# The opening of a fused three-layer kernel, entered by halves of the tokens

## The chip, the cores and the metric

The kernel runs on one core of one Trainium2 chip. The metric is the device time of one execution in microseconds (us). The engines of the core are TensorE (PE, with its weight loads PEld), VectorE (DVE), ScalarE (ACT), GpSimd (POOL) and SyncE (SP); each works through its own instructions in order, and they meet through semaphores.

## The reference, cut to what matters

The program takes 512 tokens of 1024 values through three transformer layers. Only the first steps matter here:

```python
h = x                                            # (1, 512, 1024), f32
xn = _rms_norm(h, norm_g[0, 0])                  # x / sqrt(mean(x*x) + 1e-6) * gain
gq, gk, gv, glr, gr, nq, kc, vc, ks, vs, kw, vw, ng = split(xn @ w_in)     # w_in: 1024 x 2856
# _gla: glog = log_sigmoid(glr @ w_gate + b_gate) / 16, cumulated over chunks of 64 tokens
# q and k are scaled by exp of that sum; then the chunked linear attention
```

The last step of the program is an RMS norm of the result, stored as (1, 512, 1024).

## The kernel before, in words

**Precision.** Every dense product is taken in three passes: a value is split into hi (rounded for TensorE) and lo (the rest), and hi·hi, hi·lo and lo·hi are added (mm3, L2149 to L2151). For x the split is made while the turned tokens leave PSUM: ACT writes x_hi = gain · turned (L778) and DVE writes x_lo = gain · turned − x_hi (L1415). For weights ACT copies w_raw to w_hi (split_hi, L726) and DVE subtracts to get w_lo (split_lo, L1382).

**Weights.** They come in tiles of 1 MB through two slots of w_raw, w_hi and w_lo. SP issues the load of tile n when w_lo of tile n−2 is made. The first tiles are E_IN = small, gq, gk, gv0, kc, ... ("small" holds the low-rank gate columns and the NSA gate columns, and comes in two pieces of 320 and 192 KB; only its second 128 columns are used).

**Order of the opening.** SP issues the four token tiles of x (128 tokens each), then the weight tiles 0 to 3 (L544 on), of which tile 2 waits for w_lo of tile 0 and tile 3 for w_lo of tile 1, then the two compression weights cmp_w1. ACT first issues ten small loads of constant rows (L851), loads its table for Sqrt (L769), takes the sums of squares of x tiles 0 and 2, and then makes w_hi of tile 0 (L878). DVE takes the sums of squares of tiles 1 and 3 (L1500), copies the turned gain columns from PSUM (L1504), and writes the normed tokens m (L1409). POOL makes w_lo of tile 0 (L636).

TensorE (from L2355) does eight matmuls on constants whose result nobody reads ("warm", L2155; each shows as two records), turns the gain rows (L2359), does eight more, turns x tiles 0 and 1 into all eight PSUM banks (8 transposes each, L2164), does six more warm ones, and turns tiles 2 and 3. Bank k then holds rows 128k to 128k+127 of x, turned, for all 512 tokens, and ACT and DVE split it in eight pieces of 512 columns, a bank each.

**The dense units.** A unit is one 128-column half of a weight tile against all tokens: 24 matmuls of 512 columns. `dense(x, middle)` runs them in order of x; `e_unit(x)` maps x to (tile, half): x = 0 is small, x = 1 the first half of gq, x = 2 the second half of small, which is only four small transposes of gate columns already computed, x = 3 the second half of gq, x = 4 and 5 are gk, x = 6 and 7 gv0 (matmuls of 256 columns). Units 0 and 1 run ahead of their w_lo: the lo-weight matmuls (L2405) come some steps behind the others (L2399, L2400).

After unit 0 TensorE turns the other constant rows (later_consts, L2367), and after unit 1 it computes the gate products (gate_scores, L2417), which need ACT's copy of unit 0 and three small loads that ACT issues after the split of x (e_loaded: w_gate, gate_rows, cmp_w2).

**The chain behind the gate products.** In its program order ACT runs split_hi(2) and take_in(1), then gate_logs (L936 to L940: bias, Abs, Exp, Ln for two blocks, with two table loads). DVE's order is fixed too: split_lo(2), then gate_sums (L1519 to L1525: min, subtract, scale, scan, difference, for two blocks), then the addition of the gate bias (L1629, in step x = 3), and only then split_lo(3), which is the w_lo of gv0 that unit 6 waits for.

The rest of the program, up to its last token tile, is not touched. In the five later places where the tokens are turned (`head(p)`), it is already done by halves of 256 tokens: `turned_hi` (L795) and `turned_lo` (L1431) split pieces of 256 columns, two to a bank, and as ACT and DVE must not read one bank at the same time, each of them waits for the other every second piece.

**The end.** The last token tile is finished in two halves: ACT scales the first (L1372) and DVE the second (L2141). Each adds to final_done, and SP stores both, one after the other, when both are done (L603).

Of the kernel before, what the change touches and what calls it, by code (L numbers as in the profile page):

```python
# [20 lines left out]
F32 = mybir.dt.float32  # L21
# [6 lines left out]
P = 128  # L28
# [78 lines left out]
def program(nc, A, out):  # L107
# [23 lines left out]
    with ctx:  # L131
# [195 lines left out]
        tail_gained, tail_rstd = sem("tail_gained"), sem("tail_rstd")  # L327

# [46 lines left out]
        def x_base(p, a):  # L375

            return DK + 2 * DK * (p - 1) + DK * a
# [22 lines left out]
        def e_unit(x):  # L400

            return {1: (1, 0), 2: (0, 1)}.get(x, divmod(x, 2))
# [88 lines left out]
        def _(sp):  # L491
# [39 lines left out]
            for t in range(NT):  # L531
                sp.dma_start(h[:, t, :], A["x"][0, t * P:(t + 1) * P, :]).then_inc(x_loaded[t], 16)
            def load_e(i):
# [13 lines left out]
            for i in range(4):  # L547
                load_e(i)
# [51 lines left out]
            ends = [(t, slice(0, D)) for t in range(3)] + [(3, slice(0, D // 2)), (3, slice(D // 2, D))]  # L600
            for i, (t, cols) in enumerate(ends):
                sp.wait_ge(final_done, 5 if t == 3 else i + 1)
                sp.dma_start(out[0].rearrange("(t p) d -> p t d", p=P)[:, t, cols], m[:, t, cols]).then_inc(stored, 16)  # L603
            sp.wait_ge(stored, 16 * len(ends))
# [3 lines left out]
        def _(pool):  # L608
# [27 lines left out]
            nc.gpsimd.tensor_tensor(used[0], used[1], used[2].bitcast(F32), ALU.subtract).then_inc(w_lo_ready, 1)  # L636

# [80 lines left out]
        def _(act):  # L718
# [55 lines left out]
            def first_hi():  # L774
# [78 lines left out]
            def row_load(first, which, count, src):  # L853
                cload(const_rows[first:first + count, which, :], src)

            cload(const_rows[0:32, 0, :], A["norm_g"].rearrange("l (f two) (k p) -> two (l f) k p", two=2, p=P)[0], gains_loaded)
            row_load(0, 1, 8, A["norm_mix_2"][0].rearrange("(k p) -> k p", p=P))
            row_load(8, 1, 8, A["norm_ffn_2"][0].rearrange("(k p) -> k p", p=P))
            row_load(16, 1, 8, A["c_2"][0].rearrange("(k p) -> k p", p=P))
            row_load(24, 1, 48, A["b_ada_2"][0].rearrange("(k p) -> k p", p=P))  # L860
            row_load(72, 1, 16, A["o_ln_g"][0].rearrange("(k p) -> k p", p=P))
            row_load(0, 2, 16, A["o_ln_b"][0].rearrange("(k p) -> k p", p=P))
            row_load(16, 2, 2, A["gla_b_gate"][0].rearrange("(k p) -> k p", p=P))
            row_load(18, 2, 4, A["gla_norm"][0])
            row_load(22, 2, 32, A["nsa_cmp_pos"][0].rearrange("x (a b) d -> (x a) (b d)", b=2))

# [4 lines left out]
            for t in (0, 2):  # L871
                act.wait_ge(x_loaded[t], 16)
                root_of(t, t, h[:, t, :], m[:, t, :])
                act.wait_ge(x_squares, t // 2 + 1)
                nc.scalar.activation(root[:, t + 1:t + 2], ss[:, t + 1:t + 2], ACT.Sqrt,
                                     bias=small[:, 22:23]).then_inc(squares, 1)
# [3 lines left out]
            first_hi()  # L880
            split_hi(1, 1, loaded(1), 0)
# [490 lines left out]
            nc.scalar.activation(m[:, 3, first], m[:, 3, first], ACT.Copy, scale=rstd[:, 11:12]).then_inc(final_done, 1)  # L1372
# [3 lines left out]
        def _(dve):  # L1376
# [34 lines left out]
            def first_lo():  # L1411
# [734 lines left out]
        def _(pe):  # L2146
# [6 lines left out]
            def warm(count):  # L2153
                for _ in range(count):
                    nc.tensor.matmul(ps[:, 7, 3 * P:4 * P], ones[:, :], ident[:, :], start=True, stop=True)  # L2155
# [813 lines left out]
```

## Time and profile before

| | |
|---|---|
| time, median of 3 runs | 1993.37 us (1993.0 to 1993.6) |
| profiled execution, its own time | 1993.1 us |
| its span, first to last instruction | 1991.3 us |
| TensorE busy | 1975.5 us, 99% of the span |
| DVE / ACT / POOL busy | 1019.7 / 694.5 / 404.9 us |
| chain that ended last | PE 94%, DVE 3%, ACT 2% |

The span is measured inside the program; the time has about 1.8 us more around it. In the timeline the columns are the start in us from the span's start, the duration in us of the merged stretch, the engine, the line, the operation and what it writes and reads, the count, and in brackets how long the engine had stood idle and who ended that. Matmuls are pipelined: each shows its whole latency (0.39 us for one of 512 columns), while the next starts 0.23 us later, so work is counted from start to start.

### The profile page before, as it was taken

To read this page: it belongs to the slowest core of one execution; us is meant where nothing else is said; L and a number is where in the kernel's file an instruction comes from. 1 tells how busy PE (TensorE), PEld (TensorE's weight loads), DVE (VectorE), ACT (ScalarE), POOL (GpSimd) and SP (SyncE) were. 2 spreads that over 40 slices of the span, in tenths; PEclk is the share of its full clock that TensorE was granted. 3 is DMA by queue.
4 is the path that set the end of the run, shared out by engine and by line. 5 is a ranking of instruction groups with operands and counts; after the bars stand their busy time and mean duration, and the time that the engine had idled before them with its cause. 6 is when DMAs were issued, how large, how long until landed. Compare 5 with 4: busy or idle time off the path is not lost.

```text
span 1991.3 us, 27158 instructions
## 1 busy us (share of the span) xinstructions
PE 1975.5 (99%) x11044; PEld 1656.8 (83%) x11044; DVE 1019.7 (51%) x1391; ACT 694.5 (35%) x1008; POOL 404.9 (20%) x212
## 2 busy tenths in 40 slices
PE   9999999999999999999999999999999999999998
PEld 7878888888888888889888888888877888888887
DVE  5468758357345336626727535642543664322435
ACT  6357643122124323315312212534434252222222
POOL 1000007686600101000669661000000200000000
PEclk9999999999999999999999999999999999999999
DMA  6221134444333232232445442232221223323231
GB/s 198 74 61 44 46 114 159 157 139 153 123 104 117 84 97 85 85 113 89 148 140 167 148 146 87 85 106 76 70 80 64 86 84 106 102 99 106 84 106 64
DMA packets 135032, 208.91 MB, mean 105 GB/s; under 512 B 6346, under 2 KB 105864, under 8 KB 134920
## 3 DMA queue, kind: packets, MB, share of 16 engines
q1 hardware_dynamic: 125952, 180.37, 28.0%
q0 software_dynamic: 6912, 25.17, 3.8%
q10 hardware_dynamic: 2056, 1.76, 0.3%
q8 instruction: 85, 1.39, 0.3%
q14 instruction: 27, 0.22, 0.0%
HBM read 205.18 MB, written 2.10 MB: 104 GB/s over the span
## 4 chain that ended last, share of the span: by engine, by line
PE 94%; DVE 3%; ACT 2%; issue 0%; POOL 0%; ACTq 0%; POOLq 0%
PE ps L2149 28%; PE ps L2151 28%; PE ps L2150 28%; PE ps L2210 1%; PE ps L2600 1%; PE ps L2203 1%; PE ps L2202 1%; PE ps L2611 1%; PE ps L2700 1%; PE ps L2173 1%; PE ps L2792 1%; PE ps L2155 0%; DVE m L1460 0%; PE ps L2589 0%; PE ps L2588 0%
## 5 line engine op out<-in xcount | busy, mean ns | idle before, releaser
L1382 DVE TENSOR_TENSOR w_lo<-w_raw,w_hi 128x2048 fp32r<-128x2048 f32 x149 | 349.9, 2349 | 569.2 <-ACT w_hi L726 569.2
L2149 PE MATMUL ps<-x_hi,w_hi 128*128 128x512 f32 x1240 | 487.8, 393 | 0.4 <-DVE w_lo L1382 0.4
L2151 PE MATMUL ps<-x_hi,w_lo 128*128 128x512 f32 x1240 | 482.9, 389 | 0.0
L2150 PE MATMUL ps<-x_lo,w_hi 128*128 128x512 f32 x1240 | 482.8, 389 | 0.0
L726 ACT ACTIVATE w_hi<-w_raw 128x2048 fp32r<-128x2048 f32 x151 | 288.9, 1913 | 536.0 <-PE ps L2151 434.9
L2149 PEld LDWEIGHTS ps<-x_hi,w_hi 128*128 128x128 f32 x1240 | 233.3, 188 | 50.0 <-issue 2.5
L2151 PEld LDWEIGHTS ps<-x_hi,w_lo 128*128 128x128 f32 x1240 | 232.8, 188 | 49.1
L2150 PEld LDWEIGHTS ps<-x_lo,w_hi 128*128 128x128 f32 x1240 | 233.0, 188 | 46.3
L2149 PE MATMUL ps<-w_hi,h_hi 128*128 128x512 f32 x688 | 267.8, 389 | 0.0
L2151 PE MATMUL ps<-w_hi,h_lo 128*128 128x512 f32 x688 | 267.7, 389 | 0.0
L2150 PE MATMUL ps<-w_lo,h_hi 128*128 128x512 f32 x688 | 267.6, 389 | 0.0
L2151 PEld LDWEIGHTS ps<-w_hi,h_lo 128*128 128x128 f32 x688 | 129.2, 188 | 27.0
L2150 PEld LDWEIGHTS ps<-w_lo,h_hi 128*128 128x128 f32 x688 | 129.2, 188 | 26.8
L2149 PEld LDWEIGHTS ps<-w_hi,h_hi 128*128 128x128 f32 x688 | 129.2, 188 | 26.5
L684 POOL TENSOR_SCALAR ada_w<-ada_w,cols 128x1024 f32<-128x1024 f32 x42 | 144.5, 3440 | 2.7 <-DMA ada_w<-in_w_ada 0.6
L1125 ACT ACTIVATE work<-ps 128x512 f32<-128x512 f32 x64 | 38.2, 599 | 234.6 <-PE ps L2151 211.2
L685 POOL TENSOR_TENSOR ada_acc<-ada_acc,ada_w 128x1024 f32<-128x1024 f32 x42 | 114.9, 2735 | 3.5
L1770 DVE TENSOR_TENSOR work<-work 128x512 f32<-128x512 f32 x64 | 76.2, 1191 | 70.7 <-ACT work L1125 70.7
L2149 PE MATMUL ps<-w_hi,x_hi 128*128 128x256 f32 (+1 forms) x288 | 95.7, 332 | 0.0
L2150 PE MATMUL ps<-w_lo,x_hi 128*128 128x256 f32 (+1 forms) x288 | 95.1, 330 | 0.0
L2151 PE MATMUL ps<-w_hi,x_lo 128*128 128x256 f32 (+1 forms) x288 | 95.0, 330 | 0.0
L713 POOL TENSOR_TENSOR gate_t<-gate_t 128x512 f32<-128x512 f32 x8 | 13.9, 1776 | 358.1 <-DVE gate_t L2047 358.1
(404 smaller groups left out, 2695.5 us busy)
## 6 DMA issues: line engine op xcount, KB each, us to landing
w_raw<-in_ffn_w SPq DMA_DIRECT2D x64, 1024.0 KB, 5.4
ada_w<-in_w_ada POOLq DMA_DIRECT2D x48, 512.0 KB, 4.1
w_raw<-in_w_ffn_in SPq DMA_DIRECT2D x22, 1024.0 KB, 5.1
w_raw<-in_w_in SPq DMA_DIRECT2D x20, 1024.0 KB, 5.4
w_raw<-in_o_w_in SPq DMA_DIRECT2D x16, 1024.0 KB, 5.4
w_raw<-in_w_ffn_out SPq DMA_DIRECT2D x11, 1024.0 KB, 4.9
w_raw<-in_e_w_in SPq DMA_DIRECT2D x9, 1024.0 KB, 5.4
w_raw<-in_o_w_out SPq DMA_DIRECT2D x8, 1024.0 KB, 4.8
```

The source lines that it names most:

```text
L684: chain.link(nc.gpsimd.tensor_scalar(ada_w[:, s, :], ada_w[:, s, :], c_col[:, k:k + 1], None, ALU.mult))
L685: chain.link(nc.gpsimd.tensor_tensor(ada_acc[:, 0, :], ada_acc[:, 0, :], ada_w[:, s, :], ALU.add))
L726: nc.scalar.activation(w_hi[:, slot, :], w_raw[:, slot, :], ACT.Copy).then_inc(w_hi_ready, 1)
L1125: nc.scalar.activation(work[:, f, :], ps[:, bank(st, q, f), :], ACT.Relu).then_inc(bank_free, 1)
L1382: nc.vector.tensor_tensor(w_lo[:, slot, :], w_raw[:, slot, :], w_hi[:, slot, :].bitcast(F32), ALU.subtract).then_inc(w_lo_ready, 1)
L1770: chain.link(nc.vector.tensor_tensor(r, r, r, ALU.mult))
L2149: nc.tensor.matmul(dst, a_hi, b_hi, start=start, stop=False)
L2150: nc.tensor.matmul(dst, a_hi, b_lo, start=False, stop=False)
L2151: return nc.tensor.matmul(dst, a_lo, b_hi, start=False, stop=stop_)
L2173: o = nc.tensor.transpose(turned_piece(p, t // 2, k)[:, c:c + P], m[:, t, k * P:(k + 1) * P], ident[:, :])
L2202: nc.tensor.matmul(dst, hi[:, k, blk], x_hi[:, k, toks], start=(k == 0), stop=False)
L2203: nc.tensor.matmul(dst, hi[:, k, blk], x_lo[:, k, toks], start=False, stop=False)
```

## The change

x is entered by halves of the tokens. Only tokens 0 to 255 are turned and split first; three dense units (small, gq first half, gq second half) run on them; in between the second half is turned, and then the three units run on tokens 256 to 511. The pieces are of 256 columns, in banks 4 to 7, two to a bank. The second half of gq now comes before the four small transposes of the gate columns (x = 2 and x = 3 are exchanged), and DVE's addition of the gate bias moves from step 3 to step 4, behind split_lo(3). With it come: nine loads of constant rows move from ACT's queue to SP's; x tiles 2 and 3 are loaded behind weight tiles 0 and 1; x tile 1 is squared and normed by ACT and DVE together; the warm matmuls are 8 and 4 where they were 8, 8 and 6; POOL makes half of w_lo of tile 1; and ACT itself stores the first half of the last token tile.

```diff
-            return DK + 2 * DK * (p - 1) + DK * a
+            return 2 * DK * p + DK * a
+        def first_piece(k):
+            c = 256 * (k // 2 % 2)
+            return ps[:, 4 + 2 * (k // 4) + k % 2, c:c + 256]
-            return {1: (1, 0), 2: (0, 1)}.get(x, divmod(x, 2))
+            return {1: (1, 0), 2: (1, 1), 3: (0, 1)}.get(x, divmod(x, 2))
@@ SP @@
-            for i in range(4):
-                load_e(i)
+            load_x(0)
+            load_x(1)
+            load_e(0)
+            load_e(1)
+            load_x(2)
+            load_x(3)
+            row_load(0, 1, 8, A["norm_mix_2"][0].rearrange("(k p) -> k p", p=P))
...
+            load_e(2)
+            sp.wait_ge(w1_lo_half, 1)
+            load_e(3)
@@ SP, the end @@
-            for i, (t, cols) in enumerate(ends):
-                sp.wait_ge(final_done, 5 if t == 3 else i + 1)
...
+            for t in range(3):
+                sp.wait_ge(final_done, t + 1)
+                sp.dma_start(out[0, t * P:(t + 1) * P, :], m[:, t, :]).then_inc(stored, 16)
+            sp.wait_ge(last_second, 1)
+            sp.dma_start(out[0, 3 * P:4 * P, D // 2:D], m[:, 3, D // 2:D]).then_inc(stored, 16)
@@ POOL @@
+            pool.wait_ge(w_hi_ready, 2)
+            second = [by8(w_, 1)[:, :, P:2 * P] for w_ in (w_lo, w_raw, w_hi)]
+            nc.gpsimd.tensor_tensor(second[0], second[1], second[2].bitcast(F32), ALU.subtract).then_inc(w_lo_ready, 1)
@@ ACT @@
+            def first_hi(a):
                 for k in range(DK):
-                    act.wait_ge(xt_done, k + 1)
-                    nc.scalar.activation(x_hi[:, k, :], ps[:, k, :], ACT.Copy, scale=col_gain[:, 0, k:k + 1]).then_inc(x_hi_ready, 1)
+                    act.wait_ge(xt_done, x_base(0, a) + k - k % 4 + (4 if k % 4 else 3))
+                    if k % 4 >= 2:
+                        act.wait_ge(x_ready, x_base(0, a) + k - 1)
+                    nc.scalar.activation(x_hi[:, k, 256 * a:256 * a + 256], first_piece(k), ACT.Copy,
+                                         scale=col_gain[:, 0, k:k + 1]).then_inc(x_hi_ready, 1)
...
+            root_of(0, 0, h[:, 0, :], m[:, 0, :])
+            act.wait_ge(x_loaded[1], 16)
+            chain.link(square_m(1, 1, h[:, 1, 0:D // 2], m[:, 1, 0:D // 2]))
+            act.wait_ge(x_squares, 1)
+            sqrt_of(1, ss[:, 15:16])
             act.wait_ge(w_loaded[0], loaded(0))
             nc.scalar.activation(by8(w_hi, 0)[:, :, P:2 * P], by8(w_raw, 0)[:, :, P:2 * P], ACT.Copy).then_inc(w_hi_ready, 1)
             act.wait_ge(consts_taken, 1)
-            first_hi()
-            split_hi(1, 1, loaded(1), 0)
+            first_hi(0)
+            act.wait_ge(w_loaded[1], loaded(1))
+            nc.scalar.activation(by8(w_hi, 1)[:, :, 0:P], by8(w_raw, 1)[:, :, 0:P], ACT.Copy).then_inc(w1_hi_half, 1)
+            nc.scalar.activation(by8(w_hi, 1)[:, :, P:2 * P], by8(w_raw, 1)[:, :, P:2 * P], ACT.Copy).then_inc(w_hi_ready, 1)
+            act.wait_ge(x_squares, 2)
+            sqrt_of(2, small[:, 22:23])
+            act.wait_ge(x_loaded[3], 16)
+            root_of(3, 3, h[:, 3, :], m[:, 3, :])
+            first_hi(1)
...
+            nc.scalar.activation(m[:, 3, first], m[:, 3, first], ACT.Copy, scale=rstd[:, 11:12]).then_inc(last_first, 1)
+            act.wait_ge(last_first, 1)
+            act.dma_start(out[0, 3 * P:4 * P, first], m[:, 3, first]).then_inc(stored, 16)
@@ DVE @@
+            square_x(1, slice(D // 2, D), EPS, 15)
             dve.wait_ge(consts_turned, 1)
             nc.vector.tensor_copy(cols[:, 0:32], ps[:, 0, 0:32]).then_inc(consts_taken, 1)
             normed(0, 0)
+            rooted(1)
+            nc.vector.tensor_scalar(m[:, 1, 0:D // 2], h[:, 1, 0:D // 2], rstd[:, 1:2], None, ALU.mult).then_inc(x1_half, 1)
+            nc.vector.tensor_scalar(m[:, 1, D // 2:D], h[:, 1, D // 2:D], rstd[:, 1:2], None, ALU.mult).then_inc(xs_ready, 1)
+            first_lo(0)
+            square_x(2, slice(0, D), 0.0, 2)
+            dve.wait_ge(w1_hi_half, 1)
+            nc.vector.tensor_tensor(by8(w_lo, 1)[:, :, 0:P], by8(w_raw, 1)[:, :, 0:P], by8(w_hi, 1)[:, :, 0:P].bitcast(F32),
+                                    ALU.subtract).then_inc(w1_lo_half, 1)
             normed(2, 2)
             normed(3, 3)
+            first_lo(1)
...
-            split_counted(1)
...
-                if x == 3:
+                if x == 4:
                     dve.wait_ge(e_loaded, 16 * 3)
-                    dve.wait_ge(bank_free, 4 + 3)
+                    dve.wait_ge(bank_free, 4 + 4)
@@ TensorE @@
-            warm(8)
-            pe.wait_ge(consts_taken, 1)
-            first_transposes()
+            warm(4)
+            first_transposed(0)
+            first_transposed(1)
...
+            def first_unit(x, a):
+                i, f = e_unit(x)
+                toks, base = slice(256 * a, 256 * a + 256), x_base(0, a)
+                hi, lo = by8(w_hi, i), by8(w_lo, i)
+                blk = slice(f * P, (f + 1) * P) if x else slice(P, 2 * P)
+                pe.wait_ge(*((w_hi_ready, 1), (w1_hi_half, 1), (w_hi_ready, 2))[x])
+                for k in range(DK):
+                    pe.wait_ge(x_ready, base + k + 1)
+                    nc.tensor.matmul(ps[:, x, toks], hi[:, k, blk], x_hi[:, k, toks], start=(k == 0), stop=False)
+                    nc.tensor.matmul(ps[:, x, toks], hi[:, k, blk], x_lo[:, k, toks], start=False, stop=False)
+                pe.wait_ge(*((w_lo_ready, 1), (w1_lo_half, 1), (w_lo_ready, 2))[x])
+                for k in range(DK):
+                    o = nc.tensor.matmul(ps[:, x, toks], lo[:, k, blk], x_hi[:, k, toks], start=False, stop=(k == DK - 1))
+                if a:
+                    o.then_inc(mm_done, 1)
+            first_unit(0, 0)
+            first_unit(1, 0)
+            first_transposed(2)
+            first_transposed(3)
+            first_unit(2, 0)
             for x in range(DENSE_E):
-                dense(x, in_the_middle)
+                if x < 3:
+                    first_unit(x, 1)
+                else:
+                    dense(x, in_the_middle)
```

Two waits inside it belong to the story: `first_transposed(2)` waits until all eight pieces of the first half are split (x_ready of 8), since it writes the same banks, and `first_transposed(1)` takes the first four blocks of x tile 1 as soon as DVE has normed half of it (x1_half).

## Rows read from the trace of the kernel before

**Rows 1.** Who waited for whom (us, times, longest), TensorE, 0 to 100 us.

```profile
PE ps L2399 <- DVE x_lo L1415: 1.0, 1, 1.0
```

**Rows 2.** The timeline of TensorE, 3 to 22 us.

```profile
3.64 3.78 PE L2155 MATMUL ps<-ident,ones 128*128 128x128 f32 x16 [3.64 <-POOL ones L625]
...
7.59 2.50 PE L2155 MATMUL ps<-ident,ones 128*128 128x128 f32 x16
...
13.02 1.91 PE L2164 MATMUL ps<-ident,m 128*128 128x128 f32 x16
15.88 0.47 PE L2399 MATMUL ps<-x_hi,w_hi 128*128 128x512 f32 x1 [0.95 <-DVE x_lo L1415]
```

**Rows 3.** The timeline, TensorE from the end of unit 1 to the first matmul of gv0.

```profile
26.11 1.98 PE L2405 MATMUL ps<-x_hi,w_lo 128*128 128x512 f32 x8
...
28.02 0.69 PE L2417 MATMUL ps<-f_row,w_gate 16*128 16x512 f32 x1
...
46.38 0.28 PE L2149 MATMUL ps<-w_hi,x_hi 128*128 128x256 f32 x1
```

**Rows 4.** The timeline, ACT and DVE behind the gate products.

```profile
29.23 0.69 ACT L936 ACTIVATE cum<-ps,cols 128x512 f32<-128x512 f32 x1 [0.51 <-PE ps L2417]
...
36.63 0.43 DVE L1519 TENSOR_SCALAR cum<-cum 128x512 f32<-128x512 f32 x1 [9.54 <-ACT t L940]
...
43.65 0.25 DVE L1629 TENSOR_TENSOR branch_gate<-branch_gate,gate_rows 128x96 f32<-128x96 f32 x1
43.82 2.28 DVE L1382 TENSOR_TENSOR w_lo<-w_raw,w_hi 128x2048 fp32r<-128x2048 f32 x1
```

**Rows 5.** The timeline, ACT and DVE, 5 to 21 us.

```profile
5.76 1.28 ACT L769 ACT_TABLE_LOAD   x1 [5.76 <-issue]
5.96 1.23 DVE L1500 CUSTOM_DVE_ANT_0 m<-h 128x1024 f32<-128x1024 f32 x1 [4.99 <-DMA h<-in_x]
...
7.70 0.19 DVE L1504 COPY cols<-ps 128x32 f32<-128x32 f32 x1 [0.51 <-PE ps L2359]
...
8.95 0.75 DVE L1409 TENSOR_SCALAR m<-h,rstd 128x1024 f32<-128x1024 f32 x1
...
12.10 1.06 ACT L878 ACTIVATE w_hi<-w_raw 128x1024 fp32r<-128x1024 f32 x1
```

**Rows 6.** The timeline of a later turn by halves (head 1), ACT, DVE and TensorE.

```profile
283.89 0.82 ACT L795 ACTIVATE x_hi<-ps,cols 128x256 fp32r<-128x256 f32 x2
...
287.34 0.88 DVE L1431 SCALAR_TENSOR_TENSOR x_lo<-ps,cols,x_hi 128x256 fp32r<-128x256 f32 x2 [0.21 <-ACT x_hi L795]
...
286.85 0.28 PE L2149 MATMUL ps<-x_hi,head_hi 128*128 128x256 f32 x1
...
292.60 0.28 PE L2202 MATMUL ps<-x_hi,head_hi 128*128 128x256 f32 x1
```

**Rows 7.** DMA issues of the opening: KB each, us from issue to landing.

```profile
h<-in_x SPq DMA_DIRECT2D x4, 512.0 KB, 5.7
...
cmp_w<-in_nsa_cmp_w ACTq DMA_DIRECT2D x1, 64.0 KB, 4.9
...
cmp_w_k<-in_nsa_cmp_w SPq DMA_DIRECT2D x1, 0.5 KB, 8.4
```

**Rows 8.** Lines 1382 and 685, 1000 to 1200 us: duration ns min/median/max, first and last start.

```profile
L1382 DVE TENSOR_TENSOR w_lo<-w_raw,w_hi x18: 2279/2291/4157, 1003.2 to 1188.2; 128x2048 fp32r<-128x2048 f32 x18
...
L685 POOL TENSOR_TENSOR ada_acc<-ada_acc,ada_w x17: 2385/2412/4225, 1001.6 to 1176.9; 128x1024 f32<-128x1024 f32 x17
```

**Rows 9.** The end: timeline of DVE and ACT, and the last store.

```profile
1987.42 0.49 DVE L2141 TENSOR_SCALAR m<-m,rstd 128x512 f32<-128x512 f32 x1
1987.48 0.72 ACT L1372 ACTIVATE m<-m,rstd 128x512 f32<-128x512 f32 x1 [0.47 <-DVE rstd L2130]
...
L603 SPq DMA_DIRECT2D out<-m x5: 332/351/432, 1977.5 to 1988.6; - x5
...
out<-m SPq DMA_DIRECT2D x1, 256.0 KB, 2.3
```

More of the change, by code:

```diff
@@ L529, in row, with load_x, row_load @@
                 sp.dma_start(row_gain[:, :], src.partition_broadcast(P)).then_inc(rows_loaded, 16)
-            for t in range(NT):
+            def load_x(t):
                 sp.dma_start(h[:, t, :], A["x"][0, t * P:(t + 1) * P, :]).then_inc(x_loaded[t], 16)
+            def row_load(first, which, count, src):
+                sp.dma_start(const_rows[first:first + count, which, :], src, allow_slow_non_contiguous=True).then_inc(consts_loaded, 16)
             def load_e(i):
@@ L598, in _ @@
             load_rows("g_down1", w_g2, 12)
[L600 to L604 removed]
+            for t in range(3):
[3 more added lines that the diff above has]
+            sp.dma_start(out[0, 3 * P:4 * P, D // 2:D], m[:, 3, D // 2:D]).then_inc(stored, 16)
+            sp.wait_ge(stored, 16 * 5)
         @block.gpsimd
@@ L2154, in warm, with first_transposed @@
                 for _ in range(count):
[L2155 to L2166 removed]
+                    nc.tensor.matmul(ps[:, 3, 3 * P:4 * P], ones[:, :], ident[:, :], start=True, stop=True)
+            def first_transposed(t):
+                if t == 1:
+                    pe.wait_ge(x1_half, 1)
+                else:
+                    pe.wait_ge(xs_ready, t + 1)
+                if t == 2:
+                    pe.wait_ge(x_ready, DK)
+                for k in range(DK):
+                    if t == 1 and k == DK // 2:
+                        pe.wait_ge(xs_ready, 2)
+                    c = (t % 2) * P
+                    o = nc.tensor.transpose(first_piece(k)[:, c:c + P], m[:, t, k * P:(k + 1) * P], ident[:, :])
+                    if t % 2:
+                        o.then_inc(xt_done, 1)
             def transposed(p, t):
@@ L2392, in dense @@
                 else:
-                    blk = slice(f * P, (f + 1) * P) if name != "small" else slice(P, 2 * P)
-                    behind = {0: 3, 1: DK}.get(x)
-                    for k in range(DK + behind if x < 2 else 0):
-                        if k < DK:
-                            if x == 0:
-                                pe.wait_ge(x_ready, k + 1)
-                            nc.tensor.matmul(ps[:, bank_, :], hi[:, k, blk], x_hi[:, k, :], start=(k == 0), stop=False)
-                            nc.tensor.matmul(ps[:, bank_, :], hi[:, k, blk], x_lo[:, k, :], start=False, stop=False)
-                        if k == behind:
-                            pe.wait_ge(w_lo_ready, i + 1)
-                        if k >= behind:
-                            kk = k - behind
-                            o = nc.tensor.matmul(ps[:, bank_, :], lo[:, kk, blk], x_hi[:, kk, :], start=False, stop=(kk == DK - 1))
-                    for k in range(DK if x >= 2 else 0):
+                    blk = slice(f * P, (f + 1) * P)
+                    for k in range(DK):
                         o = mm3(ps[:, bank_, :], hi[:, k, blk], lo[:, k, blk], x_hi[:, k, :], x_lo[:, k, :],
```

68 lines of the change are left out of this document (26 added, 42 removed).

## The prediction

> **What bounds the kernel.** TensorE is busy for 99% of the span, so only what changes TensorE's order, its waits or the ends of the program can change the time. I read first who waits for whom on TensorE in the first 100 us: two entries, its wait for the constants before 3.64 [rows 2] and 1.0 us for the first piece of x_lo [rows 1]. So from 15.88 us, where the first dense matmul starts [rows 2], TensorE is never short of work, and the change must pay by starting that work earlier. The timeline says what TensorE does before: warm matmuls (the groups at 3.64 and 7.59 are 8 each, two records a matmul) and the transposes, 16 of them from 13.02 [rows 2]. What sets 15.88 is the string x tile, square, root, norm, turn, split.
>
> The third reading is the one that decides here: what stands closest behind TensorE without being a wait. The gate products start at 28.02 [rows 3]; from them ACT makes the gate logarithms from 29.23, DVE sums them from 36.63, and DVE's next instruction of weight is the w_lo of gv0, 43.82 to 46.10 [rows 4]. TensorE starts on gv0 at 46.38 [rows 3], and its last gq/gk work runs right up to there. So that chain, 18.1 us from gate product to w_lo, is already exactly as long as TensorE's work beside it: its slack is nil, and no view of waits shows it.
>
> **The start of the first unit.** The table load moves from 5.76 to about 3.6, when ACT has no more row loads to issue and the constants are there (TensorE's first warm matmul started on them at 3.64). That buys less than it seems, because DVE copies the gain columns at 7.70, behind TensorE's eight slow warm matmuls, before it may norm anything [rows 2, 5]. DVE then norms x tile 0 at 8.1 in place of 8.95 [rows 5], ending at 8.85. TensorE has done its four warm matmuls by about 9.05 (16 records took 2.50 here, four matmuls are 8 of them, most at the slower pace of the first group). Eight transposes at 0.11 each (16 took 1.91 with the latency of the last [rows 2]) end at 9.9, and the third of x tile 1 at 10.25, so x_hi starts at about 10.4. From the first hi to the last lo, eight 256-column pieces took 288.22 − 283.89 = 4.33 us in a later turn of the same form [rows 6]; the first lo ends some 0.95 after its hi starts, so the first matmul starts at about 11.5 in place of 15.88, 4.4 us earlier. The weights should not hold it: x tile 1 was there at 5.96, and ACT split the small tile at 12.10 when two more x tiles had landed before it [rows 5]; the x tiles took 5.7 us at the median, issued within 1.5 us [rows 7], and without the last two in front I estimate the small tile at 8.2.
>
> **What the halves cost TensorE.** A 256-column matmul costs (292.60 − 286.85)/48 = 0.120 us [rows 6], a half unit 24 of them, 2.88. Then, step by step:
> - small, first half: paced by x_lo until 10.4 + 4.33 + 0.15 = 14.9; with its last pair and the eight lo matmuls it ends at 16.05.
> - gq first block, first half: 18.95. ACT's half of w_hi is ready at 15.2, DVE's w_lo half at 17.1 (after the 1.22 us square of x tile 2), before they are used.
> - the 16 transposes of tiles 2 and 3: 20.7. They are now work that TensorE does on the path, 1.75 us.
> - gq second block, first half: 23.6. Meanwhile the second half is split, from 20.3 to 24.6, always ahead of its use.
> - small, second half: 26.5; constant rows 0.4: 26.9; gq first block, second half: 29.75.
>
> So the gate products can start at 29.75, not at 28.02: TensorE does half a unit more (gq second block) and the transposes before them. **They come 1.7 us later although everything begins 4.4 us earlier.** TensorE's own work to gv0 is then the 18.36 of before [rows 3] less the half unit already done, 18.36 − 2.72 + 0.16 = 15.8, so it could be at gv0 at 45.5, 0.9 earlier. But the chain is a string of fixed operations behind the gate products, so w_lo of gv0 is ready at 29.75 + 18.1 − 0.2 (the gate bias addition now behind it) = 47.65, and TensorE starts gv0 at about 47.8: **1.4 us later** than 46.38. It should wait there some 2.3 us. All that follows hangs on TensorE or moves with it.
>
> **The loads.** Nine row loads leave ACT's queue for SP's; SP has them behind x tiles 2 and 3, which ACT and DVE need at 14.7 and 16.6, and ahead of tile 2, for which it waits until 12.0 anyhow; at some 0.4 each they end in time, cost nothing, and would cost up to their length if the small tile's w_lo came sooner. The three gate loads move the other way: ACT issues them only when its split of the second half runs out, the cmp_w2 one at about 24.4, and the 4.9 us of before [rows 7] puts it at 29.3, 0.45 before its use. Its ends are 0 and, with the 8.4 us that a compression load took [rows 7], which now overlap it, +3.0; I take 0, the nearer row being the same transfer.
>
> **DVE beside POOL.** POOL now makes half of a w_lo from 16.3 on while DVE makes the other and norms tiles 2 and 3. DVE's w_lo took up to 4157 ns against 2291, and POOL's two-input operation up to 4225 against 2412 in a stretch where both worked [rows 8], so the cost lies between 0 and 1.9 us on DVE, of which 0.8 is slack; I take 0. The Trainium skill (SBUF — State Buffer, "SBUF: two separate sides") says that DVE and GpSimd share a port pair as an exclusive lock. By it the norm of tile 2 would wait for the rest of POOL's operation, and the sum would come out about 1 us higher.
>
> **The end.** The two halves of the last tile end at 1987.91 on DVE and 1988.20 on ACT, but SP issues the last store at 1988.6, and it lands 2.3 us later [rows 9]. Issued by both queues at once the later one goes at about 1988.3: −0.3 to −0.4. I take −0.4; no gain if ACT's issue is as slow as its own first, and no more than 1988.6 − 1987.9 = 0.7.
>
> **Sum**, against the profiled execution's own 1993.1 (its span 1991.3): +1.4 − 0.4 = +1.0, so 1994.1. The median of the runs is 0.3 above that execution; I say 1994.3.
>
> **Rivals.**
> 1. *The chain does not hold gv0*, since ACT or DVE runs it faster than before. For it: gate_logs stood in no queue before. Against: the brackets of rows 4 show ACT ended by TensorE and DVE by ACT, so nothing was left to gain. It gives −0.9 − 0.4: 1992.0. Even this, the most that the change can give here, is far from what the 4.4 us promise.
> 2. *TensorE's clock* (the slower side). The first 16 warm records took 3.78 us, the next 16 2.50 [rows 2]: the engine came from 1.2 to 2.4 GHz only during the second group. The change takes 10 of 22 warm matmuls away, and then offers transposes and a unit that runs 0.24 us in every 0.54. If it stays at or falls to 1.2 GHz until the gq unit runs densely, the eleven transposes cost 1.2 more, the eight lo matmuls 1.0 and gq's 24 2.9: +5.0 at the gate products, 1999.2. It decides from the point where the first half unit is still at 0.21 us a matmul. Against it: before, TensorE did only transposes from 13.2 and stood idle to 15.88, and the matmuls came at full pace. The Trainium skill (TensorE: Matmul & The Clock Gate, Part 4) says that transposes do not count as activity for the clock, which speaks for this rival.
> 3. *cmp_w2 comes late*: gate products and chain +3.0, 1997.3.
> 4. *The first half is not ready earlier*, because the small tile lands behind its estimate. From 10.4 on each us of delay is a us; at the old 12.10 plus its split, 13.2, the sum is 1997.1.
>
> **Chances.** The forecast 0.62, rival 1 0.14, rival 2 0.10, rival 3 0.08, rival 4 0.06. A measurement of this kernel tells about 0.2%, 4.0 us. Forecast and rival 1 lie within it; of 2, most lies beyond; 3 and 4 with a little more on top reach it in part. Faster 0.02, same 0.87, slower 0.11. The range leaves out rival 2 and goes from the best of rival 1 to rivals 3 and 4: 1992.0 to 1997.2.
>
> **What will show it.** Right: the first x_hi·w_hi matmul near 11.5; gate products near 29.8; then a new wait of TensorE of 2 us or more for w_lo of gv0 and gv0 at about 47.8; the last store issued near 1988.3 shifted by 1.4. Wrong: gate products before 28.4 (then the change gains); no wait at gv0; 256-column matmuls at 0.21 (the clock); a wait of the gate products for a load; x_hi starting after 11.

## The result and the profile after

The kernel after took 1997.18 us (median of 16 runs, 1996.60 to 1999.38), the kernel before, run beside it, 1993.27 us (16 runs, 1992.93 to 1993.65): ratio 1.0021, 95% interval [1.0015, 1.0028]. The interval leaves out 1, so it is slower, by 3.9 us. The forecast was "within 0.2%" and +1.0, with a range up to 1997.2: the time came out at the range's upper end, and the loss is four times the one forecast.

| | before | after |
|---|---|---|
| profiled execution, its own time | 1993.1 us | 1997.16 us |
| its span | 1991.3 us | 1995.2 us |
| first dense matmul | 15.88 | 11.19 |
| gate products start | 28.02 | 32.19 |
| first matmul of gv0 | 46.38 | 50.17 |
| last matmul | 1984.02 | 1988.21 |

The first dense matmul came even 0.3 us earlier than predicted. The loss against the forecast is made between there and the gate products. Who waited for whom, TensorE, 0 to 60 us, after (us in total, times, longest; it answers to [rows 1]):

```profile
PE ps L2194 <- POOL ones L653: 3.6, 1, 3.6
PE ps L2463 <- DMA cmp_w<-in_nsa_cmp_w: 1.6, 1, 1.6
PE ps L2451 <- DVE x_lo L1448: 1.1, 3, 0.7
PE ps L2208 <- DVE m L1441: 0.8, 1, 0.8
```

Two of these were not forecast: 1.6 us in which the gate products wait for cmp_w2 (the trace calls it cmp_w), and 0.8 us in which the transposes of tile 2 wait for its norm. The predicted one, for w_lo of gv0, is missing. The timeline of TensorE after, with the same columns as [rows 2, 3]:

```profile
11.19 0.36 PE L2451 MATMUL ps<-x_hi,w_hi 128*128 128x256 f32 x1 [0.69 <-DVE x_lo L1448]
...
19.55 1.97 PE L2208 MATMUL ps<-ident,m 128*128 128x128 f32 x16 [0.76 <-DVE m L1441]
...
32.19 1.98 PE L2463 MATMUL ps<-f_row,w_gate 16*128 16x512 f32 x4 [1.58 <-DMA cmp_w<-in_nsa_cmp_w]
...
50.17 0.39 PE L2188 MATMUL ps<-w_hi,x_hi 128*128 128x256 f32 x1
```

Where the 0.76 comes from, the timeline of DVE and POOL shows (it answers to [rows 8]; each line is an instruction's start and duration in us):

```profile
15.46 1.22 DVE L1546 TENSOR_TENSOR w_lo<-w_raw,w_hi 128x1024 fp32r<-128x1024 f32 x1
15.85 3.09 POOL L667 TENSOR_TENSOR w_lo<-w_raw,w_hi 128x1024 fp32r<-128x1024 f32 x1 [3.82 <-ACT w_hi L906]
...
16.79 2.71 DVE L1441 TENSOR_SCALAR m<-h,rstd 128x1024 f32<-128x1024 f32 x1
...
19.60 0.75 DVE L1441 TENSOR_SCALAR m<-h,rstd 128x1024 f32<-128x1024 f32 x1
```

The same norm takes 2.71 us for tile 2 and 0.75 for tile 3. The first runs from inside POOL's subtraction to 19.50, shortly after POOL ends at 18.94. The DVE subtraction at 15.46, beside the same POOL instruction, kept its 1.22, but it had started first, and here POOL is the slower one: 3.09 us in place of 2.37, the 0.72 more being nearly the 0.83 for which it ran beside DVE's. So the order of the starts decides and not the operation. Two pairs out of the stretch of [rows 8] show it for the subtraction too, timeline of DVE and POOL before:

```profile
1014.09 2.29 DVE L1382 TENSOR_TENSOR w_lo<-w_raw,w_hi 128x2048 fp32r<-128x2048 f32 x1 [7.90 <-ACT w_hi L726]
1014.41 4.22 POOL L685 TENSOR_TENSOR ada_acc<-ada_acc,ada_w 128x1024 f32<-128x1024 f32 x1
...
1176.91 2.39 POOL L685 TENSOR_TENSOR ada_acc<-ada_acc,ada_w 128x1024 f32<-128x1024 f32 x1
1177.30 4.16 DVE L1382 TENSOR_TENSOR w_lo<-w_raw,w_hi 128x2048 fp32r<-128x2048 f32 x1 [8.59 <-ACT w_hi L726]
```

The one that starts first keeps its own time, the other takes 1.8 to 1.9 us more.

The load: ACT issued it 0.85 us later than the 24.4 of the prediction (0.76 of that is the wait for the norm, since the split of the second half stands behind it), and it took 2.0 longer than the 4.9 of [rows 7]. Timeline of ACT's queue, and the DMA issues of 24 to 36 us (KB, us to landing):

```profile
24.38 0.37 ACTq L888 DMA_DIRECT2D w_gate<-in_gla_w_gate  x1
24.79 0.44 ACTq L888 DMA_DIRECT2D gate_rows<-in_nsa_gate_b  x1
25.25 0.46 ACTq L888 DMA_DIRECT2D cmp_w<-in_nsa_cmp_w  x1
```

```profile
cmp_w<-in_nsa_cmp_w ACTq DMA_DIRECT2D x1, 64.0 KB, 6.9
```

25.25 + 6.9 = 32.15, and TensorE starts at 32.19. The predicted wait is missing because TensorE itself had become slow. Busy time, granted clock, DMA share and GB/s by windows of TensorE:

```profile
28.00:31.00 3.00, 2.61 (x22) 1.00 1.07 277
31.00:33.00 2.00, 0.81 (x2) 1.00 0.03 7
33.00:34.00 1.00, 1.00 (x3) 1.00 0.71 90
34.00:36.00 2.00, 2.00 (x10) 0.55 1.06 373
36.00:38.00 2.00, 2.00 (x13) 0.60 0.37 119
38.00:40.00 2.00, 2.00 (x15) 1.00 0.00 0
```

Behind the wait and the four gate matmuls, which use 16 rows, the clock falls to 1.2 GHz for 3.4 us. That used up the slack that TensorE had against the chain of w_lo, which ends at the same moment (47.83 + 2.28 = 50.11, against 50.17). Timeline of DVE, the chain (it answers to [rows 4]):

```profile
40.80 0.43 DVE L1558 TENSOR_SCALAR cum<-cum 128x512 f32<-128x512 f32 x1 [8.63 <-ACT t L970]
...
47.83 2.28 DVE L1414 TENSOR_TENSOR w_lo<-w_raw,w_hi 128x2048 fp32r<-128x2048 f32 x1
```

The end answers to [rows 9]: the stores go out from two queues, the last 4.2 us behind the last matmul (1992.42 − 1988.21), where SP alone issued it 4.6 behind (1988.6 − 1984.02). From the last matmul to the end of the span it is 7.0 us in place of 7.3.

```profile
1992.13 0.33 SPq L631 DMA_DIRECT2D out<-m  x1
1992.42 0.36 ACTq L1404 DMA_DIRECT2D out<-m  x1
```

### The profile page after: what moved, and what is told of

It reads as the page before. It is cut to its first block, busy times and chain, and to the rows that moved or that the text cites. A ratio compares the mean times of both kernels' runs of the same rounds, so it can differ in the third digit from the quotient of the medians.

```text
span 1995.2 us, 27296 instructions
## 1 busy us (share of the span) xinstructions
PE 1977.1 (99%) x11096; PEld 1660.2 (83%) x11096; DVE 1022.6 (51%) x1400; ACT 697.6 (35%) x1019; POOL 411.5 (21%) x213
## 4 chain that ended last, share of the span: by engine, by line
PE 93%; DVE 4%; ACT 2%; issue 0%; DMA 0%; POOL 0%; ACTq 0%; POOLq 0%
PE ps L2188 28%; PE ps L2190 28%; PE ps L2189 28%; PE ps L2254 1%; PE ps L2654 1%; PE ps L2247 1%; PE ps L2246 1%; PE ps L2665 1%; PE ps L2754 1%; PE ps L2217 1%; PE ps L2846 1%; DVE m L1493 0%; PE ps L2642 0%; PE ps L2643 0%; ACT ps L792 0%
```

## The experiments

There are three groups of kernels, each run on one chip with its own runs of the kernel before: 1993.09 us in the first two groups, 1993.28 in the third. Each kernel has 11 runs. The kernel after was run again in the second group only, so "below the kernel after" means below 1997.18 or 1997.19 throughout. A profiled execution is one of the 11. Where the text says "gates" and "gv0", it means the starts of the first gate matmul and of the first gv0 matmul in the profiled execution.

### First group: one cause at a time

**Gate loads early.** The three gate loads go ahead of the splits of the second half.

```diff
+            cload(w_gate[HD:HD + RANK, :], A["gla_w_gate"][0], e_loaded)
+            cload(gate_rows[:, :], A["nsa_gate_b"][0].partition_broadcast(P), e_loaded)
+            cload(cmp_w2[:, :, :], A["nsa_cmp_w2"][0].rearrange("x h d -> h x d"), e_loaded)
             act.wait_ge(x_squares, 2)
             sqrt_of(2, small[:, 22:23])
...
             first_hi(1)
-            cload(w_gate[HD:HD + RANK, :], A["gla_w_gate"][0], e_loaded)
...
```

> The changed kernel with one edit: ACT issues the three loads that the gate products wait for ahead of its split of the second half of the tokens, in place of behind it. Theory A (the gate products at 32.19 waited 1.6 us for the last of these loads, and the fixed chain behind them, 17.9 us to w_lo of gv0, sets when TensorE starts gv0 at 50.17): the gate products start near 30.6, gv0 near 48.6, the time falls by 1.5 to 1.7 us to about 1995.6. Theory B (the weight chain does not matter; TensorE's half units at the low clock level from 34.2 to 37.6 set 50.17): the same 1.6 us come back only if the low clock goes away too; if it stays, gv0 comes 1.6 us earlier as well, but w_lo is then ready well before it. Rival (another load or ACT's copy of unit 0 holds the gate products): less than 0.5 us.

Measured: 1995.71 us (1995.31 to 1996.54), ratio 1.0013 [1.0004, 1.0022]; 1.5 below the kernel after. The load takes 3.0 us, the gates at 31.59 wait for nothing, and the clock does not fall. They did not come at the expected 30.6 because this execution's first dense matmul started at 12.26, 1.07 later than in the one of after; counted from it they come 19.33 us behind in place of 21.00, 1.67 less. Now the predicted wait for w_lo is there. Timeline of TensorE:

```profile
31.59 1.98 PE L2463 MATMUL ps<-f_row,w_gate 16*128 16x512 f32 x4
```

```profile
49.58 0.38 PE L2188 MATMUL ps<-w_hi,x_hi 128*128 128x256 f32 x1 [1.48 <-DVE w_lo L1414]
```

**POOL later.** POOL makes its half of w_lo of tile 1 only when DVE has normed all tiles.

```diff
             pool.wait_ge(w_hi_ready, 2)
+            pool.wait_ge(xs_ready, 4)
```

> The changed kernel with one edit: POOL's subtraction for the second half of tile 1 waits until DVE has normed the x tiles 2 and 3. Theory (the norm of tile 2 took 2.71 us in place of 0.75 because POOL's two-input operation ran beside it): both norms take 0.75, the wait of TensorE before the transposes at 19.55 (0.8 us) goes, POOL's operation takes 2.4 in place of 3.1, and the gate products move earlier only if their load has landed, which it has not (it lands at 32.1, its issue hangs on the split of the second half, which starts earlier by the same 0.8): 0.5 to 0.8 us less, 1996.4 to 1996.7. Rival (the norm is slow for another reason, the DMA writes of x or the weights): the norm still takes 2 us or more and nothing moves.

Measured: 1996.22 us (1995.51 to 1998.05), 1.0016 [1.0007, 1.0025]; 1.0 below, a little more than the 0.5 to 0.8 expected. POOL's subtraction, now at 18.75, takes 2.38 us and both norms 0.76 and 0.75; the transposes at 18.83 wait for nothing. So it was POOL's instruction that slowed the norm, and not the DMA writes, the rival of the expectation. The load is still late. Timeline of TensorE:

```profile
18.83 1.91 PE L2209 MATMUL ps<-ident,m 128*128 128x128 f32 x16
...
31.18 1.98 PE L2464 MATMUL ps<-f_row,w_gate 16*128 16x512 f32 x4 [1.35 <-DMA cmp_w<-in_nsa_cmp_w]
```

**w_lo before block 1.** DVE makes the w_lo of gv0 between the gate sums of the two blocks, so that it waits for 3.5 us of sums less.

```diff
-            def gate_sums():
+            def gate_sums(blocks):
...
-                for b_ in range(2):
+                for b_ in blocks:
...
                 if x == 2:
-                    gate_sums()
+                    gate_sums((0,))
+                if x == 4:
+                    gate_sums((1,))
```

> The changed kernel with one edit: DVE makes w_lo of gv0 between the two blocks of its gate sums, not behind both. It is then ready near 46.7 in place of 50.1. If the chain alone sets the start of gv0, TensorE starts it 2 us or more earlier. If TensorE, slowed by the low clock level in its half unit and by the late gate products, arrives at gv0 at 50.0 of itself, as its own rows say (34.09 to 50.17 without a pause), nothing moves: 1997.1 within 0.3. I expect the second, since the two ended within 0.1 us of one another.

Measured: 1996.12 us (1995.63 to 1999.36), 1.0018 [1.0009, 1.0027]; 1.1 below. The expectation, that nothing moves within 0.3, was missed. In the profiled execution it holds nearly: w_lo starts at 44.06, 3.8 earlier than after, but gates to gv0 shrinks only from 17.98 to 17.85, since here the clock fell from 33.8 to 37.2 and TensorE was late by itself. But this execution took 1996.76. The six of the eleven runs whose mean granted clock is 1.000 took 1995.63 to 1996.12; a fall of 3.4 us at half clock, as in the profiled one, does not fit into that mean. They decide the median. That gv0 came earlier in them is likely but not shown, since none of them was profiled.

**The same, and the clock held.** Seven warm matmuls ahead of the wait for the gate loads.

```diff
             def gate_scores():
+                pe.wait_ge(consts_taken, 3)
+                warm(7)
                 pe.wait_ge(e_loaded, 16 * 3)
```

> As the run before (w_lo of gv0 between the two blocks), and in TensorE's 1.6 us wait for the load it does seven warm matmuls. If the low clock level after that wait is the second cause that ties with the chain, the half unit at 34.1 takes 2.9 us in place of 4.6, TensorE comes to gv0 near 48.5 and finds w_lo there: 1.5 to 1.8 us less than the changed kernel, about 1995.5. If the clock is not the cause: the same time as the run before, or up to 0.3 more for the warm matmuls.

Measured: 1995.64 us (1995.17 to 1996.31), 1.0012 [1.0003, 1.0021]; 1.55 below. The clock does not fall, and gates (33.09) to gv0 (49.43) is 16.3 us against 17.85. So a fall costs TensorE 1.5 us here, and it is seen in the time only where the chain of w_lo is not the later one. (The gates are late, at 33.09, with the first dense matmul, which started at 12.19 here.)

### Second group: all at once, and the parts that were taken as gains

**The kernel after, unchanged**, since its profiled execution had the fall and the predicted wait was to be seen without one.

> The changed kernel itself, unchanged, on the chip and in the rounds of the three runs beside it. Its time should be 1996.6 to 1997.5 with some runs near 1999.3. Theory of the clock: how long the opening takes depends on when the clock rises after the first warm matmuls, and on whether it falls again in the wait for the gate loads; the profile shows the level fall near 34 us in some executions only.

Measured: 1997.19 us (1996.69 to 1999.50), 1.0022 [1.0013, 1.0031], the same as in the result. In this profiled execution (1997.63) the clock did not fall; the gates start at 32.68. Waits of TensorE, 0 to 60 us, and its timeline at gv0:

```profile
PE ps L2188 <- DVE w_lo L1414: 1.5, 1, 1.5
PE ps L2463 <- DMA cmp_w<-in_nsa_cmp_w: 1.3, 1, 1.3
```

```profile
50.66 0.39 PE L2188 MATMUL ps<-w_hi,x_hi 128*128 128x256 f32 x1 [1.47 <-DVE w_lo L1414]
```

With the fall or without it gv0 comes 18.0 us behind the gates (50.66 − 32.68 and 50.17 − 32.19).

**All three**: loads early, POOL later, w_lo between the blocks (the diffs above together).

> The changed kernel with the gate loads early, POOL's subtraction behind the two norms, and w_lo of gv0 between the two blocks of the gate sums: the three things that I hold responsible for the loss. Gate products 18.6 us behind the first matmul (21.0 in the changed kernel), gv0 another 16.1 behind them with no wait: 45.9 to 46.9, against 50.17 and against 46.38 of the kernel before. Time 1992.6 to 1993.6, no slower than the kernel before. If something else costs the time (the half-width units themselves, the loads), it stays 1 us or more above the kernel before.

Measured: 1993.04 us (1992.60 to 1993.76), 1.0000 [0.9991, 1.0009]; 4.15 below the kernel after on the same chip. That is more than the sum of the three alone (1.47 + 0.96 + 1.06 = 3.5). The third part is no cost that the prediction left out but takes away the wait that it had forecast; the kernel with the first two parts only, which would have to come out at the forecast, was not run. Timeline of TensorE:

```profile
29.88 1.98 PE L2466 MATMUL ps<-f_row,w_gate 16*128 16x512 f32 x4
```

```profile
46.23 0.28 PE L2191 MATMUL ps<-w_hi,x_hi 128*128 128x256 f32 x1
```

Behind the first dense matmul TensorE waits here only for pieces of x_lo, and it still reaches gv0 only 0.15 us before the kernel before [rows 3].

**The end alone**, on the kernel before: the stores of the last tile from two queues (the part of the change's diff on SP, and ACT's and DVE's last lines).

> The kernel before with one part of the change: ACT stores the first half of the last token tile itself, SP the second. Expected 0.3 us less (last store issued 0.2 to 0.4 us earlier after the last scaling). Rival: ACT's issue is slower than SP's and nothing is gained.

Measured: 1993.15 us (1992.66 to 1993.89), 0.9999 [0.9990, 1.0009]. Last matmul to the end of the span: 7.04 us against 7.31. The medians cannot tell 0.3 us. A by-product: here the clock rose at 9.29 us, not 8.57, and the first dense matmul started at 16.23, not 15.88.

**The end and the row loads** on the kernel before: the nine row loads go to SP's queue, between weight tiles 1 and 2.

```diff
-            row_load(0, 1, 8, A["norm_mix_2"][0].rearrange("(k p) -> k p", p=P))
...
             for i in range(2):
                 load_e(i)
+            row_load(0, 1, 8, A["norm_mix_2"][0].rearrange("(k p) -> k p", p=P))
...
+            for i in range(2, 4):
+                load_e(i)
```

> The kernel before with the two parts of the change that touch no order of TensorE: the nine row loads on SP's queue (behind weight tile 1) in place of ACT's, and the two stores from two queues. The table load then starts at 2.1 in place of 5.8, DVE norms tile 0 near 8.1 in place of 8.95, tile 3 near 12.2 in place of 12.7, the first matmul near 15.3 in place of 15.88, and all behind it moves with it: 0.5 us, with the stores 0.8 us, 1992.3. Rival: the last x tile, which lands at 9.9, or DVE's own work sets the start, then the first matmul stays at 15.8 and only 0.3 is gained.

Measured: 1992.59 us (1991.93 to 1993.46), 0.9997 [0.9988, 1.0006], so 0.5 below the kernel before, not clear of noise. DVE norms its first tile at 8.01 in place of 8.95, but the transposes of tiles 2 and 3 start at 12.92 in place of 13.02 and the first dense matmul at 15.78 in place of 15.88: TensorE's own warm matmuls stand in front. The expected 15.3 was missed, and neither the last x tile nor DVE, the rivals named, is what holds it. The earlier table load is worth 0.1 us of opening here.

### Third group: the slack of the chain, and the gaps of the first unit

**The kernel before with a longer chain**: one memset more on DVE, linked between the gate logarithms and the sums.

```diff
                     dve.wait_ge(gla_pre, b_ + 1)
+                    if b_ == 0:
+                        chain.link(nc.vector.memset(state[:, 0, :, :], 0.0))
```

> The kernel before, with one memset of DVE of about 1 us linked into the gate sums of the first block, ahead of the w_lo of gv0; nothing is changed on TensorE. Theory (the chain behind the gate products has no slack in the kernel before): w_lo of gv0 starts near 44.8 in place of 43.82, TensorE shows a new wait for it of 0.9 to 1.1 us, gv0 starts near 47.4 in place of 46.38, and the time rises by 0.9 to 1.0, to about 1994.0. Rival (there was slack, and the kernel after lost its time elsewhere): w_lo moves by 1, gv0 and the time stay. The bound of what the medians can tell is some 0.5 us, so that the trace's gv0 decides.

Measured: 1994.35 us (1994.08 to 1995.14), 1.0006 [0.9997, 1.0015]; 1.1 above the kernel before, about as expected, but the interval holds 1, and the trace has to decide. Waits of TensorE, 0 to 60 us, then the timelines of DVE and TensorE:

```profile
PE ps L2151 <- DVE w_lo L1382: 0.8, 1, 0.8
```

```profile
37.13 0.91 DVE L1520 MEMSET state<- 128x1024 f32 x1 [9.80 <-ACT t L940]
...
45.27 2.29 DVE L1382 TENSOR_TENSOR w_lo<-w_raw,w_hi 128x2048 fp32r<-128x2048 f32 x1
```

```profile
28.28 0.69 PE L2419 MATMUL ps<-f_row,w_gate 16*128 16x512 f32 x1
...
47.61 0.38 PE L2151 MATMUL ps<-w_hi,x_hi 128*128 128x256 f32 x1 [0.80 <-DVE w_lo L1382]
```

From the gates to w_lo it is 16.99 us against 15.80, 1.19 more; to gv0 19.33 against 18.36, 0.97 more. So the kernel before had 0.2 us of slack there (the 1.19 is the memset's 0.91 and the link to the next instruction). The prediction had inferred this tie from two rows, since no view of waits showed it; here the wait appears as soon as the chain is longer.

**All three, and the lo matmuls between the pieces**: in the first half of unit 0 the eight matmuls with w_lo run three steps behind instead of at the end.

```diff
+                behind = 3 if x == 0 and a == 0 else DK
+                for k in range(DK + behind):
+                    if k < DK:
...
+                    if k >= behind:
+                        kk = k - behind
+                        o = nc.tensor.matmul(ps[:, x, toks], lo[:, kk, blk], x_hi[:, kk, toks], start=False, stop=(kk == DK - 1))
```

> The kernel after with the three parts (gate loads early, POOL's half w_lo behind the norms, w_lo of gv0 between the gate blocks), and in the first half of unit 0 the eight lo-weight matmuls put between the pieces, three steps behind, in place of behind all of them. Theory (of the start won, a part is lost because TensorE is paced by the pieces of x, with gaps of 0.2 to 0.3 us that the lo matmuls can fill, and w_lo of the small tile is there at 12.5): unit 0's first half ends some 0.55 us earlier (15.5 in place of 16.1 counted from a first matmul at 11.5), the transposes and all behind them too if DVE has normed tile 2 by then (17.8 or so, which it had with 1 us of slack), gates at 29.3, gv0 without a wait at 45.7, time 1992.5 against the 1993.0 of the three parts alone. Rival (something else ties TensorE before gv0, such as the weights' w_lo halves or the second half's pieces): a wait appears at the second unit or the second half, gv0 stays at 46.2, time 1993.0.

> The three parts without the lo matmuls between, unchanged from the run before, on the chip of this call: 1993.0, gv0 at 46.2 to 46.6 without a wait. It is what the run with the lo matmuls between is compared with.

Measured: 1992.29 us (1992.20 to 1993.33), 0.9996 [0.9987, 1.0005], with the lo matmuls between; 1993.24 (1992.81 to 1993.60), 1.0000 [0.9991, 1.0009], without. Counted from the first dense matmul (11.41 and 11.76) the transposes start after 6.95 and 7.44 us and gv0 after 34.23 and 34.71: 0.5 us gained, as the gaps promised, and no new wait. The medians differ by 0.95, more than that. The two profiled executions differ by 0.82 (1992.56 and 1993.38), of which 0.35 lies in the first dense matmul, which moves with the clock's rise (7.32 and 8.82 us), and the rest is the 0.5. Timeline of TensorE with the lo matmuls between:

```profile
29.30 1.98 PE L2470 MATMUL ps<-f_row,w_gate 16*128 16x512 f32 x4
```

```profile
45.64 0.28 PE L2191 MATMUL ps<-w_hi,x_hi 128*128 128x256 f32 x1
```

It is the fastest median of the study, 1.0 us under the kernel before beside it, but its interval holds 1, so it is not shown to be faster.

## Why the prediction was wrong, step by step

- **The first matmul** (11.5; 11.19): right. The time of the clock's rise moves it, from 10.99 (risen at 6.47) to 12.26 (risen at 9.86) in the executions profiled, so that a part of the agreement is luck.
- **TensorE's sum to the gate products** (29.75; 32.19): its own work was right. With the late load and the slow norm taken away the gates start at 29.88, from a first matmul at 11.53: 18.35 us, where I had 18.25. After has 21.00. The 2.65 between are the two costs that I put at nothing: 1.67 for the load, which is what the kernel with the load early gains, and 0.98 for the norm beside POOL, which is the rest. (The brackets show a little less, 1.58 and 0.76, since the last matmul's latency runs on into the wait.) The start, 0.31 early, hid a part of it, so that 2.44 is left.
- **"I take 0, the nearer row being the same transfer" is the first step that failed.** The ends 0 and +3.0 were right, the choice was not. The 4.9 us of [rows 7] was one draw, and the lowest: in before's own place the same 64 KB took 4.9, 5.0, 6.7 and 6.7 us in the four kernels with before's opening, each time covered. In after's place they took 6.6 to 6.9 us in five kernels and executions, issued early 3.0, and 3.6 to 4.0 in the three kernels with all parts together. Even issued at the 24.4 of the prediction, 6.7 us would have ended at 31.1, 1.35 too late. What makes the load long was not tested. In after the DMA engines are fully busy until 31 us, at 277 GB/s from 28 on, but with the loads early they are so until 16.6 too (share 1.06 to 1.08 from 14.6 on), and in before, where the load took longer than that, their share was only 0.54 in its first three microseconds. The rows' 0.45 us of margin was less than the spread, so rival 3 (0.08) deserved the larger part of the chance.
- **"DVE beside POOL ... I take 0" is the second.** The row from far away (up to 4157 ns for DVE against 2291) had the cost at its true size: 1.87 us, and the norm lost 1.96. What decides is who starts first, as the pairs of 1014 and 1177 us show; the prediction had POOL start at 16.3 and the norm at about 17.2, so that by its own numbers the norm would stand until 18.7: some 1.5 us, of which its slack of 0.8 covers only a part (an estimate). By after's rows the slack was 1.2, since a norm of 0.75 would have ended at 17.54 and TensorE was ready at 18.79, and it covered as much of the 1.96. The Trainium skill (SBUF — State Buffer, "SBUF: two separate sides") says that the two engines share a port pair as an exclusive lock; the sentence on it in the prediction had put this at about 1 us on the sum, and the trace shows 1.96 on the norm, of which 0.76 shows as TensorE's wait. The trace agrees with that page, and moving POOL's instruction by 3 us took the cost away.
- **The chain** (17.9 us from the gates to the end of w_lo; 17.92 from 32.19 to 50.11): right, and with it the claim that everything that delays the gates delays gv0. Nil slack measured as 0.2.
- **The wait of TensorE at gv0** (2.3; 1.5 in the executions without a fall): right in kind. TensorE needs 16.35 us from gates to gv0 where I had 15.8; 0.36 of it are the four small transposes (39.02 − 38.66 in after), which before ran among the gate products.
- **The clock** was a rival at its wrong place. The first half unit ran at full pace in each execution; the fall came behind the wait at the gates, which the prediction did not have, and it cost nothing in after, where the chain of w_lo ends at the same moment. The Trainium skill (TensorE: Matmul & The Clock Gate, Part 4) says that transposes do not count as activity; the granted clock stayed at 2.4 GHz through the 16 transposes at 19.55 and the 0.76 us of waiting before them, so that rule did not decide here.
- **The end** (−0.4): −0.3 in the profile, in no median.
- **The sum.** Against 1994.1: gv0 +2.4, the end +0.1, 0.4 that arises between gv0 and the last matmul, and 0.2 more time around the span (1.96 against 1.8): 3.1, and 1997.16 was measured. Of the 0.4, 0.28 arises at one place: in the fifth turn by halves one ACT piece comes late, in the trace of after and of all eight kernels and executions that share its opening, and in none of the four with the opening of before. The rows of after, timeline of ACT:

```profile
1625.20 0.56 ACT L829 ACTIVATE work<-ps,col_bias,cols 128x256 f32<-128x256 f32 x1
...
1627.05 0.56 ACT L829 ACTIVATE work<-ps,col_bias,cols 128x256 f32<-128x256 f32 x1 [0.38 <-DVE x_lo L1462]
```

These are 1.85 us apart, where the steps before them are 1.57. ACT waits there for DVE's piece; why it does so in these kernels only was not tested.

- **How the failure came about.** Both unseen costs delay the same point, so they add up; I had made the one a rival of its own and left the other to the ends of a term, as if only one thing could go amiss. The forecast's 1994.3 and the two together make 1996.7, just short of the 1997.4 where "within 0.2%" ends; the 0.4 that nobody had priced took it to that bound. A chance of 0.87 had no room for two small misses together. The forecast also took 0.2% for what a measurement can tell; the 16 runs told 1.0021 to within 0.0007.
- **The 4.7 us of head start** went, then, even without the two unseen costs: to transposes that before ran ahead of the first matmul and now stand between units (1.7), to the pieces that pace the first half (16.07 − 11.53 = 4.5 us for 2.9 us of matmuls, so 1.7, of which 0.5 could be filled; before lost 0.7 in the same way, so 1.0 more), to half a unit more before the gates (2.9), and to the narrower matmuls (four half units at 2.88 are 11.5 us, two units of 24 matmuls of 512 columns at 0.2275 are 10.9: 0.6). From the first matmul to the gates it is 18.35 us in place of 12.14: 6.2 more. Behind the gates stands the string of ACT and DVE, which no earlier start shortens.

**Still open.** Runs at 1998.8 to 1999.5 appear in after (3 of 16, and 2 of 11) and in the kernel with w_lo between the blocks alone (2 of 11), one at 1998.05 where only POOL was moved; none appears in the kernels whose gates do not wait for a load, or that warm TensorE ahead of it. The mean granted clock of each run points the same way: six of the seven near 1999 have 0.997 and the seventh 0.998, and so have the three slowest of the kernel with only POOL moved (1997.21, 1997.25 and 1998.05: 0.997, 0.997, 0.998), while all others have 0.998 to 1.000. Over a span of 1995 us 0.997 stands for 5 us lost or more, and the 0.999 of after's profiled execution, its fall included, for 3 at most. So the clock was low for longer in the runs at 0.997; where in the program is not known, since none of them was profiled.

## What to carry to other kernels

An earlier start pays only up to the first fixed string behind it: find the instruction whose end lies within a few tenths of a use without being a wait, and measure its slack by putting one microsecond into it. Where a moved load keeps a margin smaller than the spread of its own duration, count it as late; where several costs were put at nothing and all delay the same point, price them together. Giving idle work to POOL is not free where DVE works beside it: ask which of the two starts first, and count the rest of its time on the other.

## What the runs showed of the hardware

- Of a DVE and a POOL operation that overlap, the one that started later stood for most of the overlap: a DVE scale of 1024 columns 2.71 us in place of 0.75, a DVE subtraction of 2048 columns 4.16 in place of 2.29, POOL's operations 3.09 in place of 2.37 and 4.22 in place of 2.41. The one that started first kept its time in each pair. The pieces of x_lo, which DVE makes from PSUM and one tensor of SBUF, were not touched: 0.88 us for two beside POOL's subtraction at 9.67, which kept its 2.37, and 0.88 without it.
- TensorE's clock rose to 2.4 GHz between 6.5 and 9.9 us in the profiled executions, by the first clock record of each trace and by the pace (the eight warm records behind the gain rows took 1.16 us in after, 2.08 in the kernel with the loads early), although the first warm matmul started at 3.63 to 3.65 in all of them; the first dense matmul moved with it by up to 1.3 us. A single profiled opening is therefore not exact to better than that.
- A wait of 1.3 to 1.6 us followed by four matmuls of 16 rows was followed by a fall to 1.2 GHz in two of the four profiled executions that had one and were not warmed (after 1.58 and 1.52, not after 1.35 and 1.27; four are too few for a rule). It cost TensorE 1.5 us.
- A 64 KB load from ACT's queue took 3.0 to 6.9 us, by where it was issued, and from one and the same place 4.9 to 6.7.
